# Second block's attentions: heads taken in pairs, their values weighted in two column halves, one store a pair

## The reference

```python
s = einsum('bqhd,bkhd->bhqk', qn, k_nope) + einsum('bqhd,bkd->bhqk', qp, k_pe)      # MLA
p = masked_softmax(s * scale, k_pos <= q_pos)
y_a = einsum('bhqk,bkhd->bqhd', p, v)
...
o = g[:, :, 0] * o_cmp + g[:, :, 1] * o_slc + g[:, :, 2] * o_win                    # NSA: three softmaxes, gated
...
y_c = softmax over the 128 best keys of an index (DSA), weighted values              # keys and values shared by the heads
...
a = where(mask, exp(log_sigmoid(z) + after), 0)                                     # stick breaking
y_d = einsum('bhqk,bkhd->bqhd', a, v)
```

## Time and profile before

| | |
|---|---|
| time, median of three runs | 3433.94 us (3432.55 to 3441.81) |
| span of the profiled execution, first to last instruction | 3430.5 us |
| time of the profiled execution outside its span | not shown apart; the three runs lie 2 to 11 us above the span |
| TensorE busy | 3280.0 us, 96% |
| VectorE busy | 1557.3 us, 45% |
| ScalarE busy | 1291.4 us, 38% |
| GpSimd busy | 330.9 us, 10% |
| stages A, B, C of the first layer of the second block | 96.0, 44.4, 23.9 us |

### The profile page before, as it was taken

The page is one execution under the profiler, slowest core; times in us unless marked ns, Lnnn a source line. Parts: engine busy times, 40 slices in busy tenths (PEclk is TensorE's granted clock), DMA queues, the critical chain, the costliest instruction groups (busy, mean ns, idle before and its releaser), DMA issues. The chain is left out here.

```text
span 3430.5 us, 37516 instructions
## 1 busy us (share of the span) xinstructions
PE 3280.0 (96%) x14880; PEld 2630.6 (77%) x14880; DVE 1557.3 (45%) x2464; ACT 1291.4 (38%) x2257; POOL 330.9 (10%) x156
## 2 busy tenths in 40 slices
PE   7999999999999999999889999999999988899998
PEld 6867678878888888877666788878887767678886
DVE  4154522244343333446975433343334388663333
ACT  3344642333232322234665423242223346642222
POOL 0411324400000000014000000000000330000000
PEclk9999999999999999999999999999999999999999
DMA  4311223323333333332002233323333310023322
GB/s 145 93 42 44 86 62 105 99 81 102 94 98 98 98 94 97 98 101 86 13 1 62 89 96 98 98 81 98 98 95 99 107 47 1 19 80 98 98 92 74
DMA packets 77070, 280.61 MB, mean 82 GB/s; under 512 B 8800, under 2 KB 9056, under 8 KB 76640
## 3 DMA queue, kind: packets, MB, share of 16 engines
q1 hardware_dynamic: 76896, 278.21, 26.6%
HBM read 276.08 MB, written 2.10 MB: 81 GB/s over the span
## 5 line engine op out<-in xcount | busy, mean ns | idle before, releaser
L539 ACT ACTIVATE w_hi<-raw_slabs 128x1024 fp32r<-128x1024 f32 x496 | 524.2, 1058 | 1247.4 <-PE ps L579 1131.3
L554 DVE TENSOR_TENSOR w_lo<-raw_slabs,w_hi 128x1024 fp32r<-128x1024 f32 x372 | 455.0, 1224 | 725.6 <-ACT w_hi L539 725.5
L579 PE MATMUL ps<-in_hi,w_hi 128*128 128x512 f32 x1840 | 720.4, 392 | 9.6 <-DVE in_lo L902 7.8
L579 PE MATMUL ps<-in_lo,w_hi 128*128 128x512 f32 x1840 | 717.5, 390 | 0.0
L579 PE MATMUL ps<-in_hi,w_lo 128*128 128x512 f32 x1840 | 717.5, 390 | 0.0
L579 PE MATMUL ps<-parts,w_hi 128*128 128x512 f32 x2240 | 693.9, 391 | 0.9 <-DVE scratch L1508 0.8
L554 POOL TENSOR_TENSOR w_lo<-raw_slabs,w_hi 128x1024 fp32r<-128x1024 f32 x124 | 306.9, 2477 | 2471.9 <-ACT w_hi L539 2471.9
L579 PEld LDWEIGHTS ps<-parts,w_hi 128*128 128x128 f32 x2240 | 420.3, 188 | 92.6 <-issue 4.3
L579 PE MATMUL ps<-parts,w_lo 128*128 128x512 f32 x1120 | 435.8, 389 | 0.0
L579 PEld LDWEIGHTS ps<-in_hi,w_hi 128*128 128x128 f32 x1840 | 346.0, 188 | 88.6 <-issue 9.1
L579 PEld LDWEIGHTS ps<-in_hi,w_lo 128*128 128x128 f32 x1840 | 346.4, 188 | 72.0
(11 more groups left out here) (277 smaller groups left out, 3498.7 us busy)
## 6 DMA issues: line engine op xcount, KB each, us to landing
raw_slabs<-weights SPq DMA_DIRECT2D x510, 512.0 KB, 3.6
big<-rope SPq DMA_DIRECT2D x2, 2304.0 KB, 8.8
x_resid<-xT SPq DMA_DIRECT2D x8, 256.0 KB, 3.9
outT<-x_resid SPq DMA_DIRECT2D x8, 256.0 KB, 2.0
const_cols<-consts SPq DMA_DIRECT2D x1, 836.0 KB, 9.0
scratch<-brow SPq DMA_DIRECT2D x1, 768.0 KB, 9.8
vector_cols<-vec SPq DMA_DIRECT2D x2, 45.5 KB, 9.4
vector_cols<-vec SPq DMA_DIRECT2D x1, 69.0 KB, 3.1
```

The source lines that it names most:

```text
L539: self.nc.scalar.activation(self.w_hi[:, m % SPLIT, :], self.raw[:, n % RAW, :], ACT.Copy)\
L554: (self.nc.gpsimd if i is None else self.nc.vector).tensor_tensor(self.w_lo[:, m % SPLIT, :], self.raw[:, n % RAW, :], self.w_hi[:, m % SP ...
L579: mm = k.nc.tensor.matmul(out, lhsT, rhs, start=(c == 0 and m == 0), stop=(last and m == 2))
```

## The change

The units of stages A, B and C are put in another order: for each pair of heads (0 and 1, 2 and 3) and block of queries, the unit of the even head and right behind it that of the odd one. `weigh` is replaced there by `weigh_pair`, called at every second step: it goes through the key blocks, and at each it weights the values of the even head with 64 stationary columns into partitions 0 to 63 of a bank, and then those of the odd head into partitions 64 to 127 of the same bank. ScalarE stores the whole bank of 128 partitions once a pair. The laid tiles have a ring of four in place of three in stages A and C (tiles 6 to 9 of the scratch), and three still in stage B. The first block's phase (heads of 128 columns) keeps its order and its functions.

```diff
+def weigh_pair(k, pair, pts, bank):
+    for j, (a, w) in enumerate(pair[0].blocks):
+        for m, (u, pt) in enumerate(zip(pair, pts)):
+            mm = k.nc.tensor.matmul(k.ps[64 * m:64 * m + 64, bank, 0:P], u.values[j], pt[0:w, a:a + P],
+                                    start=(u.first and j == 0), stop=(u.last and j == len(u.blocks) - 1))
+    return mm
+def attend_pairs(k, pe, u, n, units, probs, ready, turned, laid, pair_done, stored):
+    if 0 <= u < n:
+        pe.wait_ge(ready, k.at(ready, u + 1))
+        if u >= 2:
+            pe.wait_ge(laid, k.at(laid, u - 1))
+        turn(k, units[u], probs(u), 3 + u % 2).then_inc(turned, 1)
+    v = u - 2
+    if 0 <= v < n and v % 2:
+        pair = units[v - 1:v + 1]
+        pe.wait_ge(laid, k.at(laid, v + 1))
+        if pair[0].first and pair[0].group >= 3:
+            pe.wait_ge(stored, k.at(stored, pair[0].group - 2))
+        weigh_pair(k, pair, [k.scr[:, 6 + i % 4, :] for i in (v - 1, v)], 5 + pair[0].group % 3).then_inc(pair_done, 1)
+def lay_and_store_pairs(k, act, u, n, units, turned, laid, pair_done, stored):
+    nc = k.nc
+    if 0 <= u < n:
+        act.wait_ge(turned, k.at(turned, u + 1))
+        if u >= 4:
+            act.wait_ge(pair_done, k.at(pair_done, (u - 4) // 2 + 1))
+        rows = units[u].blocks[0][1]
+        cols = P * len(units[u].blocks)
+        nc.scalar.activation(k.scr[0:rows, 6 + u % 4, 0:cols], k.ps[0:rows, 3 + u % 2, 0:cols], ACT.Copy)\
+            .then_inc(laid, 1)
+    w = u - 3
+    if 0 <= w < n and w % 2 and units[w].last:
+        act.wait_ge(pair_done, k.at(pair_done, w // 2 + 1))
+        nc.scalar.activation(units[w].out, k.ps[:, 5 + units[w].group % 3, 0:P], ACT.Copy).then_inc(stored, 1)
...
-    groups = sum(1 for u in units if u.last)
+    per = 2 if paired else 1
+    groups = sum(1 for u in units if u.last) // per
+    advance, settle = (attend_pairs, lay_and_store_pairs) if paired else (attend, lay_and_store)
     with k.block() as block:
...
-                if 0 <= i - 4 < n:
+                if 0 <= i - 4 < n and i % 2:
                     u = i - 4
                     pe.wait_ge(laid, k.at(laid, u + 1))
-                    if u >= 2:
-                        pe.wait_ge(stored, k.at(stored, u - 1))
-                    weigh(k, units[u], laid_at(u), out_bank(u)).then_inc(unit_done, 1)
+                    if u // 2 >= 2:
+                        pe.wait_ge(stored, k.at(stored, u // 2 - 1))
+                    weigh_pair(k, units[u - 1:u + 1], [laid_at(u - 1), laid_at(u)], out_bank(u // 2)).then_inc(pair_done, 1)
...
-                if 0 <= i - 5 < n:
+                if 0 <= i - 5 < n and i % 2 == 0:
                     u = i - 5
-                    lo, hi = units[u].rows
-                    act.wait_ge(unit_done, k.at(unit_done, u + 1))
-                    nc.scalar.activation(units[u].out, k.ps[lo:hi, out_bank(u), 0:P], ACT.Copy).then_inc(stored, 1)
+                    act.wait_ge(pair_done, k.at(pair_done, u // 2 + 1))
+                    nc.scalar.activation(units[u].out, k.ps[:, out_bank(u // 2), 0:P], ACT.Copy).then_inc(stored, 1)
                 if i < n:
...
                     if u >= 3:
-                        dve.wait_ge(unit_done, k.at(unit_done, u - 2))
+                        dve.wait_ge(pair_done, k.at(pair_done, (u - 3) // 2 + 1))
                     nc.vector.tensor_copy(laid_at(u)[:, 0:cols], k.ps[:, turn_bank(u), 0:cols]).then_inc(laid, 1)
...
     units = []
-    for h in range(HEADS):
+    each = P // dims
+    for h0 in range(0, HEADS, each):
         for qb in range(QB):
-            w = P * (qb + 1)
-            pairs = scores(h, qb) if scores else [(q(h)[:, P * qb:P * qb + P], key(h)[:, 0:w])]
-            pairs += extra(h, w) if extra else []
-            lo = 64 * (h % 2) if dims == 64 else 0
-            units.append(Unit(pairs, w, [v(kb, h) for kb in range(qb + 1)], QB * h + qb, True, True,
-                              (lo, lo + dims), out(h)[lo:lo + dims, P * qb:P * qb + P], masks(qb), scale))
+            for h in range(h0, h0 + each):
+                w = P * (qb + 1)
+                pairs = scores(h, qb) if scores else [(q(h)[:, P * qb:P * qb + P], key(h)[:, 0:w])]
+                pairs += extra(h, w) if extra else []
+                units.append(Unit(pairs, w, [v(kb, h) for kb in range(qb + 1)], QB * (h0 // each) + qb, True, True,
+                                  (0, P), out(h)[:, P * qb:P * qb + P], masks(qb), scale))
     return units
...
-    shared = lambda col: (lambda kb, h: v_tok(kb)[:, col - 64 * (h % 2):col - 64 * (h % 2) + P])
+    shared = lambda col: (lambda kb, h: v_tok(kb)[:, col:col + 64])
     others = softmax_units(lambda h: tile(25 + h), lambda h: tile(29 + h),
-                           lambda kb, h: v_mla[:, kb, P * (h // 2):P * (h // 2) + P], 64, causal, ys(0))
+                           lambda kb, h: v_mla[:, kb, 64 * h:64 * h + 64], 64, causal, ys(0))
     units = []
-    for h in range(HEADS):
-        lo = 64 * (h % 2)
+    for h0 in range(0, HEADS, 2):
         for qb in range(QB):
             wd = P * (qb + 1)
-            more = dict(group=2 * (QB * h + qb), rows=(lo, lo + 64), out=ys(1)(h)[lo:lo + 64, P * qb:P * qb + P])
-            gate = lambda b: gates[:, qb, 4 * b + h:4 * b + h + 1]
-            qs = two_heads(14)(h)[:, P * qb:P * qb + P]
-            units.append(Unit([(qs, kc[h % 2])], wide, [vc], first=True, last=False, gate=gate(0),
-                              mask=k.mask("cmp_neg")[:, wide * qb:wide * (qb + 1)], **more))
+            more = dict(group=2 * (QB * (h0 // 2) + qb), rows=(0, P), out=ys(1)(h0)[:, P * qb:P * qb + P])
+            gate = lambda b, h: gates[:, qb, 4 * b + h:4 * b + h + 1]
+            qs = lambda h: two_heads(14)(h)[:, P * qb:P * qb + P]
+            units += [Unit([(qs(h), kc[h % 2])], wide, [vc], first=True, last=False, gate=gate(0, h),
+                           mask=k.mask("cmp_neg")[:, wide * qb:wide * (qb + 1)], **more) for h in (h0, h0 + 1)]
 
 
             for b, (kt, col) in enumerate(((ks, VS0), (kw, VW0))):
-                units.append(Unit(in_halves(h, qb, kt), wd, [shared(col)(kb, h) for kb in range(qb + 1)],
-                                  first=False, last=(b == 1), gate=gate(b + 1), mask=causal(qb), **more))
-            one = others[QB * h + QB - 1 - qb]
-            one.group = more["group"] + 1
-            units.append(one)
-    attention_phase(k, units, select, range(TOP_CUTS[0], TOP_CUTS[2]))
+                units += [Unit(in_halves(h, qb, kt), wd, [shared(col)(kb, h) for kb in range(qb + 1)],
+                               first=False, last=(b == 1), gate=gate(b + 1, h), mask=causal(qb), **more)
+                          for h in (h0, h0 + 1)]
+            at = 2 * (QB * (h0 // 2) + QB - 1 - qb)
+            for one in others[at:at + 2]:
+                one.group = more["group"] + 1
+                units.append(one)
+    attention_phase(k, units, select, range(TOP_CUTS[0], TOP_CUTS[2]), paired=True)
     units = softmax_units(two_heads(21), lambda h: tile(sk[h // 2][h % 2]),
-                          lambda kb, h: v_tok(kb)[:, VB0 + P * (h // 2):VB0 + P * (h // 2) + P], 64,
+                          lambda kb, h: v_tok(kb)[:, VB0 + 64 * h:VB0 + 64 * h + 64], 64,
                           lambda qb: k.mask("strict"), ys(3))
 
     stick_phase(k, units, select, range(TOP_CUTS[2], TOP_STEPS * (QB - 1)))
     units = softmax_units(None, None, shared(VD0), 64,
                           lambda qb: causal(0) if qb == 0 else k.parts[:, INDEX_AT[qb], 0:P * (qb + 1)], ys(2),
                           scores=lambda h, qb: in_halves(HEADS + h, qb, dk))
-    attention_phase(k, units)
+    attention_phase(k, units, paired=True)
```

More of the change, by code:

```diff
@@ L1911, in lay_and_store, with attention_phase @@
         nc.scalar.activation(one.out, k.ps[lo:hi, 5 + one.group % 3, 0:P], ACT.Copy).then_inc(stored, 1)
-def attention_phase(k, units, index=None, steps=range(0), lead=None, first=0):
+def attention_phase(k, units, index=None, steps=range(0), lead=None, first=0, paired=False):
     nc = k.nc
@@ L1937, in _ @@
                     score(k, units[i], bank(i)).then_inc(scored, 1)
-                attend(k, pe, i - lag, n, units, probs, probs_ready, turned, laid, unit_done, stored)
+                advance(k, pe, i - lag, n, units, probs, probs_ready, turned, laid, unit_done, stored)
         @block.vector
@@ L1981, in _ @@
                         lead.scalar(act, i)
-                lay_and_store(k, act, i - lag, n, units, turned, laid, unit_done, stored)
+                settle(k, act, i - lag, n, units, turned, laid, unit_done, stored)
     k.passed(scored=n, row_max=n, bias_scaled=scaled[-1], probs_expd=n, row_inv=n, probs_ready=n,
-             turned=n, laid=n, unit_done=n, stored=groups, top8=len(steps), top8_taken=len(steps),
+             turned=n, laid=n, unit_done=n // per, stored=groups, top8=len(steps), top8_taken=len(steps),
              select_made=rows_done(steps))
```

(10 more changed lines are left out.)

## The result

| | before | changed |
|---|---|---|
| median | 3433.58 us (20 executions) | 3440.14 us (20 executions) |
| ratio, 95% interval | | 1.0015 [1.0009, 1.0022] |
| span of the profiled execution | 3430.5 us | 3439.6 us |

The ratio makes it 3 to 8 us slower, about 5. That is inside the 0.3% that I called no change, but the median lies 0.1 us above my range, and its sign is the other one. (The medians stand 6.6 us apart; single executions of each kernel scatter by 10 to 15 us, so I go by the ratio's interval.)

The account below looks back on a forecast made before the run. VectorE was taken to bound stage A, a loop with no full engine B, TensorE C. A -0.7, B -1.0 and C -0.9 made -2.6 us a layer, -5.2 for two: 3433.9 to 3428.7 us, 8-in-10 range 3414 to 3440.

Parts of the forecast that it names:

- Part 1: Weighing in two column halves, stages A to C: halves overlap, so a pass takes 0.055 us instead of 0.111.
- Part 2: Weighing in A, B and C: going into the column halves and out again costs 0.44 us a visit.
- the first rival: Visits are free: entering and leaving the halves costs nothing; -8.5 us a layer, 3417 us; chance 0.33.
- C's term: Stage C (DSA), set by TensorE: 4.4 us saved by halves, 3.5 paid for visits, -0.9 us a layer.
- The tail of C: End of stage C: 18 passes today, then 28 half passes with two visits, growing from 2.0 to 2.4 us.
- rival of free visits: Same as the first rival; its terms were C -3.4, A -2.3, B -2.8 us a layer; chance 0.33.
- Part 3: One store a pair: saves ScalarE 2.0 us a layer in B and in C; 0.5 taken in B, nothing elsewhere.
- The sum for A (-0.7) and B (-1.0): Per layer, us: A, half of 1.4 of VectorE's waits; B, half of TensorE's -0.9, and -0.5 for stores.
- part 4: Order and waits in A, B, C: between nothing and one more 1.2 us VectorE wait per stage; nothing taken.
- the order eats it: Rival: one more 1.2 us wait each in B and C from equal widths side by side; about 3433.5 us; chance 0.15.
- The clock: Sign of being wrong: a stage's clock falls from its 0.97 to 1.00 as TensorE does less.
- No overlap: Rival, slower: halves don't overlap, a pass keeps 0.111 us, each visit costs 0.44; +6.2 a layer, 3446 us; chance 0.12.

Follow-up runs that it names:

- e7: Changed kernel with all weighing products of a pair's even head, then all of the odd head's, instead of by turns; 3444.43 us, ratio 1.0024.
- e1: Kernel before with the pair order in all three stages, but full-width weighing and one store a unit; 3441.81 us, ratio 1.0017.
- e3: Kernel before with pairs in stage A alone, B and C as before; 3439.72 us, ratio 1.0006.
- e12: Kernel before with pairs in stage C alone, a second run of the same kernel as e2; 3436.23 us, ratio 1.0003.
- e14: Kernel before with stage B's blocks of queries from 512 keys down to 128, no pairs; 3432.21 us, ratio 0.9992.
- e10: Kernel before with the query blocks of stage A's NSA heads from 512 keys down to 128; 3448.22 us, ratio 1.0027.
- e4: Kernel before with pairs in stage B alone, A and C as before; 3439.69 us, ratio 1.0010.
- e13: Kernel before with pairs in stages B and C, B's from 512 keys down, A as before; 3427.82 us, ratio 0.9980.
- e2: Kernel before with pairs in stage C alone, A and B as before; 3432.60 us, ratio 0.9991.

## Why the prediction was wrong, step by step

- **Part 1, 0.055 a pass:** right, 0.054 to 0.055, and e7 shows that the alternation is needed for it beyond four passes a head.
- **Part 2, the visit:** there and of the kind of the earlier trace rows, so the first rival falls; mis-sized, 0.32 to 0.35 in place of 0.44. With it C's term is 4.4 - 8 x 0.34 = 1.7 in place of 0.9 us: measured 1.5, and TensorE's busy time fell from 22.16 to 20.56. The tail of C, said to grow from 2.0 to 2.4, shrank, from 2.37 to 1.96 for the 28 passes: both last pairs are weighed in one run, with one visit and not two.
- **A slip in the rival of free visits:** 5.22 - 4.2 is 1.0, not 0.85, so its C would be -4.1 and its sum -9.2 a layer. It changes nothing in the outcome.
- **Part 3, stores:** right in number and size. What they are worth in B wasn't measured apart from the halves, nor was the fourth laid tile in A and C.
- **The sum for A (-0.7) and B (-1.0):** measured +1.7 and +2.2, and +2.2 twice. The step that failed is the last sentence of part 4, "I take nothing", for the order of the units. e1 gives the order's price without halves and without the shared store: +2.6 and +2.1 in A, +1.6 and +1.8 in B. I had it as a rival, *the order eats it*, but priced it at one wait of 1.2 us in B and C and exempted A, "VectorE 90% busy whatever the order". It is the reverse: A and B pay, C pays nothing.
- **The clock:** I named its fall as what would make me wrong and argued it away: "B holds 1.00 today at a busy share of 0.80". That was a mean over a stage. The falls that I cut out stand behind single stretches with TensorE busy 1.22, 1.68 and 1.83 of 3.40 us, which such a mean hides. With the order alone (e1) A has 18 us at the lower level in place of 5, and with order and halves 25. That stretches at the lower level lengthen a stage is shown on equal instructions: e3's A (+2.6 us for 6 us more of it), e12's A (+2.2 for 8), e14's A (+1.3 for 6), the old B of e3 and e10 against before's (+1.2 to 1.5 for 3.4), and the paired C (24.1 with none, 25.7 to 25.9 with 6 to 7).
- **How much of the order's price is clock:** not settled in A. At 0.2 to 0.44 us for each microsecond at the lower level, by these, the 14 us more of e1's A are worth 3 to 6 us, more than the 2.6 and 2.1 that it lost, so nothing else is needed; but no run had the pair order in A with the clock of before. In B the answer is clearer: with 3 us at the lower level it takes 45.6 to 45.9 us in the old order (e3, e10), 46.0 and 46.2 in the pair order at full width (e1) and 45.7 and 45.9 with halves (e4), so with equal time at the lower level neither moves it by more than 0.6. Nor did the halves fail: on a line between e3's 94.9 (15) and the change's 97.9 (25), the paired A would take about 96 at e1's 18 us, some 2 less than e1 took. That is an estimate. What stays open is why the clock falls in one stage and holds in another on equal instructions, as in B of before and of e3, or in A of before and of e12.
- **No overlap:** falls by the passes; e7 shows that without alternation it would have been 0.087 a pass in the mean of the widest pairs, since two heads still share four passes' time.

## What to carry to other kernels

What a change takes off TensorE, or gains by another order of its work, can be paid back by its clock: read the granted clock and the busy time in stretches of a few microseconds, above all at the start and end of a stage, not the stage's mean. Price the order of the work apart from the work saved, and try it alone first; here the order outweighed the halving of every pass. In a stage whose steps hang on each other, such as B, try the narrowest unit last, and take a saving only in the stages where it doesn't lower the clock (here C, and B with wide pairs first, though then C pays).

## What the hardware showed that I had not expected

- Half-width f32 products of one half that follow each other step by 0.109 us, as full ones do, but at the change from one half to the other about four passes of each overlap, without any alternation in the program (e7).
- Entering column halves costs 0.13 to 0.15 us and leaving 0.19 to 0.20. The Trainium skill, TensorEngine Tiling, Key Properties, says that a change of mode drains TensorE; the trace agrees, with these numbers.
- The code ahead of the second block's stage A is the same in all kernels here, but its time moves: stage A starts at 1653.4 us in the profile of before, at 1654.3 in e1 and 1655.1 in e13, and at 1659.3 in the changed kernel, 1662.5 in e2 and 1662.6 in e12, with 26, 26, 36, 47, 53 and 53 us at the lower level ahead of it. That is the size of the scatter of before's 20 times, 3431.5 to 3441.8, and more than C's whole gain of 3 us, so a gain of that size has to be read from its stage.
